# A decoder in one launch on one Trainium2 core: three norm transitions, from 128x512 tiles to 128x4 tiles

## What is computed

```
def rmsnorm_2(x, g):
    xf = x.astype(jnp.float32)
    y = xf * lax.rsqrt(jnp.mean(xf * xf, axis=-1, keepdims=True) + NORM_EPS)
    return (y * g.astype(jnp.float32)).astype(x.dtype)

def modulate(h, shift, scale):
    return h * (1 + scale[:, None, :]) + shift[:, None, :]
...
        x = x + g_m[:, None, :] * rmsnorm_2(y, norm_g[l, 1])
        h = modulate(rmsnorm_2(x, norm_g[l, 2]), sh_f, sc_f)
        y = squared_relu_mlp(h, mlp_up_w[l], mlp_down_w[l])
        x = x + g_f[:, None, :] * rmsnorm_2(y, norm_g[l, 3])
```

## Time and profile before

| what | us |
|---|---|
| median of 3 runs (lowest, highest) | 1772.66 (1772.09, 1772.86) |
| the profiled execution, its own time | 1770.3 |
| its span, first to last instruction | 1768.5 |
| PE busy | 1742.3 (99% of the span), weight loads 1410.2 |
| DVE busy | 1104.8 (62%) |
| ACT busy | 637.4 (36%) |
| POOL busy | 99.3 (6%) |

### The profile page before, as it was taken

One profiled execution on the slowest core, in us unless ns is written; L12 is line 12 of the kernel. 1 busy time (PEld: TensorE's weight loads), 2 busy tenths in 40 slices (PEclk: granted clock), 3 DMA queues, 4 the chain that ended last, 5 costly groups with the idle time before them and its releaser, 6 DMA issues. The chain is left out here.

```text
span 1768.5 us, 22712 instructions
## 1 busy us (share of the span) xinstructions
PE 1742.3 (99%) x8136; PEld 1410.2 (80%) x8136; DVE 1104.8 (62%) x1626; ACT 637.4 (36%) x997; POOL 99.3 (6%) x158
## 2 busy tenths in 40 slices
PE   9999999999999999999999999998999999999998
PEld 8877677888888888887888888876767788888887
DVE  7766555655555576878656565678775865434355
ACT  5236544322222353244413141444445441323241
POOL 0000000000000000100100000002000100000001
PEclk9999999999999999999999999999999999999999
DMA  7321112444444434652255556431321225333231
GB/s 242 110 97 37 37 51 70 152 167 143 145 175 147 140 104 140 219 179 84 83 180 188 204 178 212 167 107 42 120 71 37 84 87 175 95 95 97 94 95 48
DMA packets 62095, 216.63 MB, mean 122 GB/s; under 512 B 7232, under 2 KB 9408, under 8 KB 61824
## 3 DMA queue, kind: packets, MB, share of 16 engines
q1 hardware_dynamic: 45216, 154.95, 25.8%
q0 software_dynamic: 16656, 60.04, 10.8%
q10 hardware_dynamic: 144, 0.59, 0.1%
HBM read 212.67 MB, written 2.10 MB: 121 GB/s over the span
## 5 line engine op out<-in xcount | busy, mean ns | idle before, releaser
L793 ACT ACTIVATE w_hi<-w_raw 128x1024 fp32r<-128x1024 f32 x283 | 297.6, 1053 | 379.7 <-PE psum L1961 343.4
L1177 DVE TENSOR_TENSOR w_lo<-w_raw,w_hi 128x1024 fp32r<-128x1024 f32 x283 | 345.9, 1222 | 117.5 <-ACT w_hi L793 109.3
L1959 PE MATMUL psum<-h_hi,w_hi 128*128 128x512 f32 x1064 | 414.8, 390 | 0.0
L1960 PE MATMUL psum<-h_lo,w_hi 128*128 128x512 f32 x1064 | 413.9, 389 | 0.0
L1961 PE MATMUL psum<-h_hi,w_lo 128*128 128x512 f32 x1064 | 413.9, 389 | 0.0
L1961 PE MATMUL psum<-hid_hi,w_lo 128*128 128x512 f32 x736 | 286.3, 389 | 0.0
L1959 PE MATMUL psum<-hid_hi,w_hi 128*128 128x512 f32 x736 | 286.3, 389 | 0.0
L1960 PE MATMUL psum<-hid_lo,w_hi 128*128 128x512 f32 x736 | 286.3, 389 | 0.0
L1959 PEld LDWEIGHTS psum<-h_hi,w_hi 128*128 128x128 f32 x1064 | 199.7, 188 | 42.3 <-issue 0.5
L1960 PEld LDWEIGHTS psum<-h_lo,w_hi 128*128 128x128 f32 x1064 | 199.7, 188 | 42.1 <-issue 0.5
L1961 PEld LDWEIGHTS psum<-h_hi,w_lo 128*128 128x128 f32 x1064 | 199.7, 188 | 41.2
(11 more groups left out here) (331 smaller groups left out, 2007.3 us busy)
## 6 DMA issues: line engine op xcount, KB each, us to landing
w_raw<-in_wstream SPq DMA_DIRECT2D x283, 512.0 KB, 3.6
ada_raw<-in_ada POOLq DMA_DIRECT2D x112, 512.0 KB, 3.8
x<-in_xT SPq DMA_DIRECT2D x8, 256.0 KB, 5.2
outT<-x SPq DMA_DIRECT2D x16, 128.0 KB, 1.8
con<-in_consts SPq DMA_DIRECT2D x1, 1028.0 KB, 9.9
w_raw<-in_wstream SPq DMA_DIRECT2D x4, 256.0 KB, 4.2
con<-in_rope ACTq DMA_DIRECT2D x1, 576.0 KB, 6.0
c_row<-in_crow POOLq DMA_DIRECT2D x1, 512.0 KB, 3.9
```

The costliest lines, as they stand in the source:

```text
L793: act.activation(w_hi[:, slot, :], w_raw[:, slot, :], ACT.Copy).then_inc(whi_done, 1)
L1177: dve.tensor_tensor(w_lo[:, slot, :], w_raw[:, slot, :], w_hi[:, slot, :].bitcast(F32), ALU.subtract).then_inc(wlo_done, 1)
L1959: pe.matmul(bank, w_hi[:, slot, w], hi[:, ra + k, :], start=k == 0, stop=False)
L1960: pe.matmul(bank, w_hi[:, slot, w], lo[:, ra + k, :], start=False, stop=False)
```

## The change

- The means are turned round. The sum tiles become stationary, 128 tokens at a time, and a matrix of 128 columns moves through, so that the mean of a token lies on a partition, and 512 tokens are four columns: `root1`, `root2`, `resum` and `x_mean` become 128x4. One moving matrix (`pick`) carries 1/1024 in one half and 0 in the other, so that the means of y^2 and g^2 y^2 lie side by side in one PSUM bank (`means`, columns 0 and 64 of each group of 128). The last chunk's square serves both: its moving matrix `gcol` has 1/1024 in one half and g^2/1024 in the other, and ACT's square of g y for that chunk goes.
- `gcol`'s second half is written by DVE in each of three `gains` stages, for the columns `r_m0`, `r_f0` and `r_m1`. There is one tile of it, and the `gains` stage of the next column stands ahead of the transition that reads it, so in transitions 0 and 1 the last chunk's share of the mean of g^2 y^2 is formed with the next column's g.
- The roots are Ln and Exp on 128x4. To bring them back to all partitions PE takes a column of the root, broadcast to 128 columns, as stationary and the identity as moving matrix, four times 128 columns: `root1` into `root_wide`, `root2` into `root_new`, and in transition 1 `root2` once more into `root_copy`, from where ACT copies it to SBUF behind chunk 2 of `renew`.
- The five stages become two, `roots` and `renew`. `keep_warm` is 3 products behind the first root's spread and 7 behind the second's (3 in transition 1, where four go to the copy), for 27.
- At the program's start DVE fills `pick` and half of `gcol` (three memsets).

```diff
@@ plan @@
-        add("sums", dict(aux=1), inst=inst)
-        rstd(EPS2, first_of=inst + 1)
-        add("resum", inst=inst, old=old)
-        rstd(EPS2, second_of=inst + 1)
+        add("roots", dict(aux=1, rstd=2), inst=inst, old=old)
@@ ACT @@
+                        if c < DT - 1:
+                            if c >= 2:
+                                act.wait_ge(g_added, 6 * inst + max(c - 2, 1))
+                            act.activation(g_sq[c % 2], y[:, c, :], ACT.Square, scale=gain_of(s["old"], c))\
+                               .then_inc(g_squared, 1)
...
+                elif kind == "roots":
+                    inst, r = s["inst"], s["at"]["rstd"]
+                    act.wait_ge(aux_done, s["at"]["aux"] + 1)
+                    act.activation(root1[:, :], mean_y, ACT.Ln, bias=eps[EPS2][:, :]).then_inc(ln_done, 1)
+                    act.wait_ge(ln_done, r + 1)
+                    act.activation(root1[:, :], root1[:, :], ACT.Exp, scale=-0.5).then_inc(rstd_done, 1)
+                    act.wait_ge(resum_done, inst + 1)
+                    act.activation(root2[:, :], x_mean[:, :], ACT.Ln, bias=eps[EPS2][:, :]).then_inc(ln_done, 1)
+                    act.wait_ge(ln_done, r + 2)
+                    act.activation(root2[:, :], root2[:, :], ACT.Exp, scale=-0.5).then_inc(rstd_done, 1)
@@ ACT, renew @@
+                        if s["inst"] == 1 and c == 2:
+                            act.wait_ge(kept_done, 1)
+                            act.activation(rstd[:, :], root_copy, ACT.Copy).then_inc(root_kept, 1)
@@ DVE, resummed @@
-                dve.wait_ge(means_done, means + 1)
-                dve.tensor_tensor(resum, mean_g, rstd[:, :], ALU.mult).then_inc(resum_step, 1)
+                dve.wait_ge(rstd_done, s["at"]["rstd"] + 1)
+                dve.tensor_tensor(resum[:, :], mean_g, root1[:, :], ALU.mult).then_inc(resum_step, 1)
...
@@ DVE, renew @@
+                dve.wait_ge(wide_done, s["inst"] + 1)
@@ DVE, gains @@
+                    for name in s["names"]:
+                        if name in OLD:
+                            g = gain_of(name, DT - 1)
+                            dve.tensor_scalar(gcol[:, HALF_P:P], mean[D][:, 0:HALF_P], g, g, ALU.mult, ALU.mult)\
+                               .then_inc(gcol_done, 1)
@@ PE @@
+            def roots(s, warm_bank):
+                inst, r, each = s["inst"], s["at"]["rstd"], mean[D][:, :]
...
+                for t in range(QB):
+                    pe.matmul(means[:, t, :], ss[:, tokens(t)], pick_y, start=t == 0, stop=False)
...
+                for t in range(QB):
+                    pe.matmul(means[:, t, :], g_sum[:, tokens(t)], pick_g, start=False, stop=False)
...
+                for t in range(QB):
+                    mm = pe.matmul(means[:, t, :], y_sq[1][:, tokens(t)], gcol[:, :], start=False, stop=t == QB - 1)
+                mm.then_inc(aux_done, 1)
+                pe.wait_ge(mul_added, 7 * (inst + 1))
+                for t in range(QB):
+                    mm = pe.matmul(mean_mul(inst)[:, t, :], mul_sum[:, tokens(t)], each, start=True, stop=True)
+                mm.then_inc(means_done, 1)
+                if inst == 0:
+                    pe.wait_ge(x_added, DT - 1)
+                    for t in range(QB):
+                        mm = pe.matmul(mean_x[:, t, :], x_sum[:, tokens(t)], each, start=True, stop=True)
+                    mm.then_inc(means_done, 1)
+                pe.wait_ge(rstd_done, r + 1)
+                for t in range(QB):
+                    mm = pe.matmul(root_wide(inst)[:, tokens(t)], root1[:, t:t + 1].broadcast_to([P, P]), ident,
+                                   start=True, stop=True)
+                mm.then_inc(root_done, 1)
+                keep_warm(ROOT_WARM, warm_bank)
+                pe.wait_ge(rstd_done, r + 2)
+                for t in range(QB):
+                    mm = pe.matmul(root_new(inst)[:, tokens(t)], root2[:, t:t + 1].broadcast_to([P, P]), ident,
+                                   start=True, stop=True)
+                mm.then_inc(wide_done, 1)
...
+                keep_warm(NEW_WARM - (QB if inst == 1 else 0), warm_bank)
```

More of the change, by code:

```diff
@@ L50 @@
 ENDS, HALF = 3, 256
-NEW_WARM = 27
+HALF_P = P // 2
+ROOT_WARM, NEW_WARM = 3, 7
 SHIFT = 1
@@ L434, in build @@
         ada_sum = sb("ada_sum", [P, ADA_ROWS])
-        x_mean = sb("x_mean", [P, S])
+        x_mean = sb("x_mean", [P, QB])
+        resum = sb("resum", [P, QB])
+        root1 = sb("root1", [P, QB])
+        root2 = sb("root2", [P, QB])
+        gcol = sb("gcol", [P, P])
+        pick = sb("pick", [P, P + HALF_P])
         par = sb("par", [P, PARAMS])
@@ L540, in build @@
         means_done = sem("means_done")
+        pick_done = sem("pick_done")
+        gcol_done = sem("gcol_done")
         root_done = sem("root_done")
+        wide_done = sem("wide_done")
+        kept_done = sem("kept_done")
         resum_step = sem("resum_step")
@@ L564, in build @@
         GAIN = dict(g_m0=0, r_m0=1, g_f0=2, r_f0=3, g_kv=4, g_m1=5, r_m1=6, g_f1=7)
+        OLD = ("r_m0", "r_f0", "r_m1")
         r_f1 = sb("r_f1", [P, DT])
@@ L667, in mean_mul @@
         def mean_mul(inst):
-            return psum[:, 0 if inst == 1 else O_BANK, :]
+            return psum[:, 0 if inst == 1 else O_BANK, :].rearrange("p (t n) -> p t n", n=P)
+        mean_x = psum[:, PT_BANK + 1, :].rearrange("p (t n) -> p t n", n=P)
+        root_copy = psum[:, 3, :]
         def new_val(inst, c):
@@ L1173, in _ @@
             dve.memset(proj[:, 8:12, :], 0.0).then_inc(zeroed, 1)
+            dve.memset(pick[:, :], 0.0).then_inc(pick_done, 1)
+            dve.wait_ge(pick_done, 1)
+            dve.memset(pick[:, HALF_P:P], 1.0 / D).then_inc(pick_done, 1)
+            dve.memset(gcol[:, 0:HALF_P], 1.0 / D).then_inc(pick_done, 1)
             def split_lo(m, slot):
@@ L1861, in _ @@
                     update(s)
-                elif kind == "resum":
+                elif kind == "roots":
                     resummed(s)
@@ L2188, in attention @@
                         begin((4, 5))
+            def roots(s, warm_bank):
+                inst, r, each = s["inst"], s["at"]["rstd"], mean[D][:, :]
+                pe.wait_ge(rstd_done, r)
+                pe.wait_ge(pick_done, 3)
+                pe.wait_ge(y_added, 6 * (inst + 1))
+                for t in range(QB):
+                    pe.matmul(means[:, t, :], ss[:, tokens(t)], pick_y, start=t == 0, stop=False)
+                pe.wait_ge(g_added, 6 * (inst + 1))
+                for t in range(QB):
+                    pe.matmul(means[:, t, :], g_sum[:, tokens(t)], pick_g, start=False, stop=False)
+                pe.wait_ge(gcol_done, inst + 1)
+                pe.wait_ge(y_squared, DT * (inst + 1))
+                for t in range(QB):
[21 more added lines that the diff above has]
+                mm.then_inc(wide_done, 1)
+                if inst == 1:
+                    for t in range(QB):
+                        mm = pe.matmul(root_copy[:, tokens(t)], root2[:, t:t + 1].broadcast_to([P, P]), ident,
+                                       start=True, stop=True)
+                    mm.then_inc(kept_done, 1)
+                keep_warm(NEW_WARM - (QB if inst == 1 else 0), warm_bank)
@@ L2292, in _ @@
                       .then_inc(twin_x, 1)
[L2293 to L2310 removed]
+                elif kind == "roots":
+                    roots(s, PT_BANK if s["inst"] == 1 else next(p for p in PLAN[idx:] if p["kind"] == "gemm")["at"]["o"] % BANKS)
                 elif kind == "total":
```

59 lines of the change are left out of this document (14 added, 45 removed).

## The result

The changed kernel takes 1761.92 us in the median of four runs (1761.63 to 1762.59), beside 1772.38 (1770.91 to 1772.86) for the kernel before on the same chip: ratio 0.9946, 95% interval 0.9934 to 0.9959: half a per cent faster, and clear of the noise. On a second chip it is 1761.82 (five runs) against 1770.92: ratio 0.995, 0.9937 to 0.9964.

What follows compares the result with a forecast made beforehand. The prediction took PE, busy 1742.3 of 1768.5 us, as occupied but not needed in transitions, where a chain through other engines sets the end. Gains of 2.4, 3.3 and 3.3 sum to 9.0: 1772.66 - 9.0 = 1763.7 us, range 1760.8 to 1768.0.

Steps and rivals of the forecast that it cites:

- E stays within 0.05: E, the start of PE's product with the last chunk's square in each transition, shifts by no more than some 0.05 us.
- A group in 0.92: On PE, a group of four float32 products of 128 columns, eight records, takes 0.92 us.
- Rival A: PE becomes the transition's bound: weight loads don't overlap, a group takes 1.5 us, the kernel 1773.9 us; chance 3%.
- Ln at E+1.2, the first root at E+1.7: On ACT, Ln starts 1.2 us after the last square's product starts on PE; the first root is ready at 1.7.
- Small steps from E+1.95 in 0.20 each: DVE's five small steps start 1.95 us after the last square's product starts, 0.20 each, 1.0 together against 3.40 before.
- First spread seen at E+3.0, in transition 0 at E+3.95: DVE waits for the first root's spread until 3.0 us after the last square's product starts, 3.95 in transition 0.
- First renew operation E+6.3, 5.4, 5.4: First `renew` operation after the last square's product starts: 6.3, 5.4, 5.4 us in transitions 0 to 2, gaining 2.4, 3.3, 3.3.
- The second spread 0.6 early: The second root's spread on PE is visible 0.6 us before DVE needs it, hidden under 2.12 us of scaling.
- The 0.40 of transition 2 kept: Transition 2's stage-boundary wait, 0.79 us and not 0.39, has an unexplained 0.40 that was assumed to stay.
- rival B: The gain is handed back or the chain isn't shortened as said; each transition gains about 1 us: 1769.7; chance 5%.
- The median 2.4 above the profiled execution: The median stands 2.4 us above the profiled execution, so the forecast is 1772.66 - 9.0 = 1763.7 us.
- rival C: PE's clock falls with fewer unread products: 2.5 us lost per fall, 1771.3, or 1798 if it lasts; chance 2%.

Runs made afterwards that it cites:

- one_col: The changed kernel with the moving matrices of the means one column wide (two for the last chunk's square) instead of 128; 1766.67 us, ratio 0.9971 to the kernel before.
- warm_nine: The changed kernel with 9 unread products instead of 3 between the two spreads of the roots; 1763.45 us, ratio 0.9958 to the kernel before.
- merge_only: The kernel before, all tiles 128x512, with its five drained stages per transition made two; 1769.36 us, ratio 0.9988 to the kernel before.
- after_again: The changed kernel unaltered, measured and profiled a second time; 1761.82 us, ratio 0.995 to the kernel before.
- no_unread: The changed kernel without any unread products in the three transitions; 1764.98 us, ratio 0.9964 to the kernel before.
- no_boundary: The changed kernel without the drain and self-wait of ACT and DVE ahead of `renew`; 1761.88 us, ratio 0.9945 to the kernel before.

## Why the prediction was right

It was right in sign, size and mechanism, at 1763.7 for 1761.92; 9.0 us forecast, 9.3 in the traces. Part of that closeness is luck: terms that were too low by 0.40 and 0.19 us and one that was too high by 0.24 partly made up for one another.

- *E stays within 0.05.* It came 0.08 later. The two groups ahead of it take 0.88 each and not 0.92; but PE starts E's group 0.14 behind ACT's square where it had been 0.06. Three times 0.08 is the only term that went against the change.
- *A group in 0.92.* Groups start 0.89 apart (828.32, 829.22, 830.11), 0.111 a record. Rival A would have had 1.5. The row that spoke against A (eight records in 0.95) has one moving column and not 128; by one_col it could stand in, since the further columns cost 0.07 a group. The Trainium skill (TensorE: Matmul & The Clock Gate, section Back-to-back issue gap) has 81 ns for a pair at 128 columns. At the higher clock level this case shows 111, so by that page a group is 0.24 too short and its sum of 10.2 too large.
- *Ln at E+1.2, the first root at E+1.7.* E+1.23 (828.58), Exp's end E+1.73.
- *Small steps from E+1.95 in 0.20 each.* DVE began at E+1.83: counted from the later E its weight split ends at E+1.62 and not E+1.71, and the boundary is 0.21. Steps are 0.19 to 0.20, the second 0.28.
- *First spread seen at E+3.0, in transition 0 at E+3.95.* E+2.98 and E+3.85.
- *Scaling, add and scaling 2.12, boundary 0.23.* From the first scaling to the first `renew` operation 833.57 - 831.20 = 2.37, of which 0.23 are the boundary.
- *First renew operation E+6.3, 5.4, 5.4.* E+6.22, 5.35, 5.34.
- *The second spread 0.6 early.* 0.75, by warm_nine.
- *The 0.40 of transition 2 kept.* The largest mis-sized term: it went, as merge_only shows, with the boundaries. The forecast terms, 8.92 unrounded, + 0.40 for it, + 0.19 for marks that came earlier than forecast, - 0.24 for E are the 9.27 of the marks.
- *Nothing handed back (rival B).* E to end shrank by 9.4 and 9.2, as much as the marks. The operations on `gcol`, the memsets and the copy of root2 cost nothing that shows.
- *The median 2.4 above the profiled execution.* This did not carry over, and is why the forecast is 1.8 us too high. Before's profiled execution (1770.3) lay below all runs of its median; after's (1762.59, with the fall at 98 us) lies 0.7 above its median, after_again's (1761.55) 0.3 below. The profiled time was forecast at 1761.3. By medians the gain is 10.5 on one chip and 9.1 on the other; for the 1.2 by which the first exceeds the marks no row gives a cause.
- *Clock 9 everywhere (rival C, 2%).* The digits are 9, and in the transitions the clock is 1.00, but for a reason the prediction did not have: it named the unread products that were cut and not what the 128 columns and those left do. Without either, in no_unread and one_col, 3.1 and 7.7 us were lost (E to end). Rival C read the low level out of the pace of the first products (36 records in 6.68 us); the granted clock of before stands at 1.00 in every window there, 0 to 8 us, so that column doesn't confirm the reading. The 0.50 of no_unread and one_col does.

## What to carry to other kernels

Before you shorten work that hides behind an idle-looking matrix engine, count how the result travels: a mean taken with the sum as stationary operand leaves four columns instead of 512 per partition, and the trip back by the identity is one short group of matmuls, whose place in PE's order then sets the chain. Try the removal of the matrix engine's filler and of its full moving width each on its own before you trust it: here both looked like waste, and without either the clock fell. Measure a change of half a per cent from a mark in the program to its end, as well as by the span.

## What was not expected of the hardware

- A group of eight float32 records takes 0.81 us when 1 column moves and 0.88 when 128 do, from its start to the next (one_col, after), and with one column the granted clock fell from 1.00 to 0.50 in each of three transitions of the profiled execution, while PE had no gap but 0.08 us in its records.
- The clock fell around PE waits of 2.73 and 2.38 us and not behind one of 1.49 (no_unread), nor behind 1.89 (before) or 0.8 to 1.0 (after). The low level cost 1.0 and 2.1 us in the stretches that held it; 128x512 matmuls in it were recorded with 0.63 us instead of 0.39.
- One more fall, at 98 us, comes in one execution of a program and not in another (after, after_again) and costs 1.4 us; its cause is open.
- Leaving out a stage boundary of which the profile shows 0.23 moved the mark by 0.32 to 0.33 each time (no_boundary).
